# Hybrid encoder trunk: deep projection banks, filled norm gaps, and the recurrent stream and queries in three products

## What is computed

```python
z = x @ w_in                       # columns: rnn stream 1024 | q 1024 | k 128 | v 128 | two gates 2048
A = rglru(causal_conv(z_rnn))      # linear recurrence over tokens
B = banded attention(rope(q), rope(k), v, sinks)
m = sigmoid(g_rnn) * (A @ w_br_rnn) + sigmoid(g_attn) * (B @ w_br_attn)
x = LayerNorm(alpha * x + m @ w_out)
scores = sigmoid(x @ w_router)     # top 8 of 64 experts, in 4 of 8 groups
x = LayerNorm(alpha * x + shared_expert(x) + sum_topk gate_e * expert_e(x))
```

## Time and profile before

| | |
|---|---|
| median of 3 runs | 1719.76 us (1717.3 to 1720.46) |
| the profiled execution | 1717.09 us |
| its span, first to last instruction | 1715.3 us |
| busy in the span | TensorE 96%, VectorE 42%, ScalarE 29% |
| layer 0: first projection product / first recurrent gate product | 15.78 / 95.29 us |
| layer 0: to_tokens / fill / router / gather | 277.54 / 286.61 / 294.33 / 322.22 us |
| layer 1: first projection product | 863.21 us |

### The profile page before, as it was taken

One profiled execution on the slowest core, in us unless ns is written; L12 is line 12 of the kernel. 1 busy time (PEld: TensorE's weight loads), 2 busy tenths in 40 slices (PEclk: granted clock), 3 DMA queues, 4 the chain that ended last, 5 costly groups with the idle time before them and its releaser, 6 DMA issues.

```text
span 1715.3 us, 24854 instructions
## 1 busy us (share of the span) xinstructions
PE 1640.0 (96%) x9230; PEld 1059.5 (62%) x9230; DVE 719.6 (42%) x1543; ACT 495.4 (29%) x1005; POOL 23.2 (1%) x38
## 2 busy tenths in 40 slices
PE   8999998999999999999799999989999999999995
PEld 5667897745545555555477779966555555545543
DVE  3646565333333323423445656562342333333323
ACT  1054434123223222232211544332223223223222
POOL 2000000000000000000010000000000000000000
PEclk9999997999999999999889999979999999999997
DMA  7644466299999999999246425554999999999960
GB/s 194 150 149 146 100 172 227 73 359 391 401 402 407 393 394 409 387 409 400 78 104 203 152 83 140 142 208 170 393 402 396 400 403 401 391 410 396 402 240 30
DMA packets 166339, 476.30 MB, mean 278 GB/s; under 512 B 43252, under 2 KB 99124, under 8 KB 133508
## 3 DMA queue, kind: packets, MB, share of 16 engines
q1 hardware_dynamic: 164480, 472.32, 73.5%
q0 software_dynamic: 1440, 2.98, 0.7%
q10 hardware_dynamic: 356, 0.13, 0.0%
HBM read 473.83 MB, written 1.57 MB: 277 GB/s over the span
## 4 chain that ended last, share of the span: by engine, by line
PE 94%; DVE 2%; ACT 2%; issue 1%; DMA 0%; POOL 0%; SPq 0%; DVEq 0%; ACTq 0%; POOLq 0%
PE ps L793 26%; PE ps L518 17%; PE ps L813 13%; PE ps L834 4%; PE ps L835 4%; PE ps L778 4%; PE ps L779 4%; PE ps L531 3%; PE ps L532 3%; PE ps L533 3%; PE ps L544 2%; PE ps L781 2%; PE ps L822 1%; PE ps L728 1%; DVE stats_of L1226 1%
## 5 line engine op out<-in xcount | busy, mean ns | idle before, releaser
L793 PE MATMUL ps<-experts,xg 128*64 128x512 f32 x2048 | 450.5, 592 | 2.8 <-ACT xg L1073 2.8
L793 PEld LDWEIGHTS ps<-experts,xg 128*64 128x64 f32 x2048 | 148.4, 137 | 293.0 <-issue 293.0
L518 PE MATMUL ps<-xT,dense 128*128 128x288 f32 x1184 | 302.7, 416 | 4.9 <-DVE tmp L1290 4.2
L518 PEld LDWEIGHTS ps<-xT,dense 128*128 128x128 f32 x1184 | 227.5, 194 | 70.3 <-issue 6.8
L813 PE MATMUL ps<-experts,hidT 128*64 128x512 f32 x1024 | 233.8, 598 | 1.8 <-ACT hidT L1087 1.8
L1507 DVE TENSOR_TENSOR hid<-ps,hid 128x256 f32<-128x256 f32 x64 | 27.2, 425 | 388.4 <-ACT hid L1081 388.4
L1095 ACT ACTIVATE yh<-ps,gsl 128x512 fp32r<-128x512 f32 x128 | 88.0, 687 | 228.2 <-PE ps L813 228.2
L1073 ACT ACTIVATE xg<-ps,gperm_all 128x256 f32<-128x256 f32 x256 | 130.6, 561 | 62.8 <-PE ps L781 59.2
L1519 DVE SCALAR_TENSOR_TENSOR yl<-ps,gsl,yh 128x512 fp32r<-128x512 f32 x128 | 96.1, 751 | 124.5 <-ACT yh L1095 124.5
L834 PE MATMUL ps<-ohT,yh 128*128 128x288 f32 x512 | 145.1, 308 | 3.1 <-DVE yl L1519 3.1
L813 PEld LDWEIGHTS ps<-experts,hidT 128*64 128x64 f32 x1024 | 68.5, 136 | 121.6 <-issue 121.6
(11 more groups left out here) (253 smaller groups left out, 1707.6 us busy)
## 6 DMA issues: line engine op xcount, KB each, us to landing
experts<-in_w SPq DMA_DIRECT2D x384, 1024.0 KB, 9.5
dense<-in_w_in SPq DMA_DIRECT2D x26, 1024.0 KB, 5.4
dense<-in_w_in SPq DMA_DIRECT2D x32, 256.0 KB, 4.4
dense<-in_w_br_rnn SPq DMA_DIRECT2D x8, 1024.0 KB, 5.2
dense<-in_w_br_attn SPq DMA_DIRECT2D x16, 512.0 KB, 6.2
dense<-in_w_out SPq DMA_DIRECT2D x8, 1024.0 KB, 5.3
dense<-in_ws SPq DMA_DIRECT2D x6, 1024.0 KB, 5.6
tok<-in_x_prompt SPq DMA_DIRECT2D x1, 1024.0 KB, 5.3
```

Of the source, the lines that this page charges most:

```text
L518: last = mm(bank[:, 0:n], w[:, k, col:col + P], rhs(k), start=k == 0, stop=k == KC - 1)
L793: last = mm(ps[e % 2 * CAP:(e % 2 + 1) * CAP, 2, :], xg[:, k, e * CAP:e * CAP + CAP], experts[:, e, 0:2, k * DE:k * DE + DE], start=k == 0 ...
```

## The change

1. **Banks.** Projection items use `z_bank(i)`: bank i % 6 up to the last query, bank i % 2 from the recurrent gates on. An item waits for item i-6.
2. **Order.** Keys and values go ahead of the queries, in products and in pieces. VectorE turns the keys first; the small tables of layer 0 come after all ropes.
3. **Three products** for stream chunks 2 to 7 and all queries, 14 chunks a layer. Seven pieces more go through `high_parts` and `low_parts`. ScalarE makes `x_hi` and VectorE `x_lo` from `xT` at the start of a layer.
4. **Fills** use all eight banks; only the first two chunks wait.
5. **Router** with the weights stationary: eight products with 288 moving columns, each as soon as its chunk is evicted, a VectorE copy into `lgT`, three transposes back.
6. **Order behind norm 1**: `xh`/`xl` of tiles 0 and 1 around the copy, of tile 2 after the sigmoid and after the gates.
7. **`keep_clock`**: matmuls of the identity by 512 columns whose result is not read: 6 behind `to_tokens(yP)`, 3 behind the last `combine`, 4 behind `to_tokens(ffT)`.

```diff
+FILL = (0, 1, 4, 5, 6, 7, 2, 3)
-Z_RNN, Z_Q, Z_K, Z_V, Z_LRU, Z_GATE, ... = 0, 8, 16, 17, 18, 34, ...
+Z_RNN, Z_K, Z_V, Z_Q, Z_LRU, Z_GATE, ... = 0, 8, 9, 10, 18, 34, ...
+Z_DEEP = 6
-PIECES = ([("in", 256 * j) for j in range(4)] + [("q", j) for j in range(4)] + [("in", K_OFF)]
+PIECES = ([("in", 256 * j) for j in range(4)] + [("in", K_OFF)] + [("q", j) for j in range(4)]
-SPLIT = list(range(D_BR, D_ROUTER))
+SPLIT = list(range(D_IN + 1, D_KV)) + list(range(D_Q, D_G)) + list(range(D_BR, D_ROUTER))
+F_BR = SPLIT.index(D_BR)
+def z_bank(i):
+    return i % Z_DEEP if i < Z_LRU else i % 2
...
             def bank_of(L, i):
-                pe.wait_ge(z_free[i % 2], z_count(L, i))
-                return ps[:, i % 2, :]
+                if Z_DEEP <= i < Z_LRU:
+                    pe.wait_ge(z_free[i % 2], z_count(L, i - Z_DEEP) + 1)
+                elif i >= Z_LRU:
+                    pe.wait_ge(z_free[i % 2], z_count(L, i))
+                return ps[:, z_bank(i), :]
...
             def fill_xT(wait):
                 for c in range(KC):
-                    wait(c)
+                    if c < 2:
+                        wait(c)
                     for t, (at, n) in enumerate(TOK):
-                        last = transpose(ps[:, c % 2, at:at + n], tok[0:n, t, c * P:c * P + P], ident[0:n, 0:n])
+                        last = transpose(ps[:, FILL[c], at:at + n], tok[0:n, t, c * P:c * P + P], ident[0:n, 0:n])
...
+            def keep_clock(bank, n):
+                for _ in range(n):
+                    mm(ps[:, bank, :], ident, cst[:, 0:512], start=True, stop=True)
...
# TensorE, a layer
+                    ready = (lambda k: pe.wait_ge(x_lo_ready, 2 * L + k // 4 + 1)) if m == 2 else None
+                    over_parts(L, bank_of(L, Z_RNN + m), D_IN + m // 2, m % 2 * P, x_hi, x_lo, ready).then_inc(z_ready[m % 2], 1)
...
+                for c in range(KC):
+                    over_parts(L, bank_of(L, Z_Q + c), D_Q + c // 2, c % 2 * P, x_hi, x_lo).then_inc(z_ready[c % 2], 1)
...
                 to_tokens(yP)
+                keep_clock(0, 6)
...
-                for t, (at, n) in enumerate(TOK):
-                    for k in range(KC):
-                        last = mm(ps[0:n, 2, t * NE:t * NE + NE], xT[:, k, at:at + n], w[:, k, :], start=k == 0, stop=k == KC - 1)
+                for k in range(KC):
+                    pe.wait_ge(z_free[k % 2], z_count(L, Z_FILL1 + k) + 1)
+                    last = mm(ps[0:NE, 0, 0:T], w[:, k, :], xT[:, k, :], start=k == 0, stop=k == KC - 1)
+                last.then_inc(logits_T, 1)
+                pe.wait_ge(logits_kept, L + 1)
+                for t, (at, n) in enumerate(TOK):
+                    last = transpose(ps[0:n, 2, t * NE:t * NE + NE], lgT[0:NE, at:at + n], ident[0:NE, 0:NE])
                 last.then_inc(logits, 1)
...
                 round_of(pe.snap(done), meanwhile=shared_down)
+                keep_clock(2, 3)
                 pe.wait_ge(rounds_set, L + 1)
...
                 to_tokens(ffT)
+                keep_clock(0, 4)
...
# ScalarE, a layer
+                for h in range(2):
+                    ...
+                    activation(x_hi[:, c, :], xT[:, c, :], ACT.Copy).then_inc(x_hi_ready, 1)
+                if L == 0:
+                    high_parts(0, 0)
+                high_parts(L, 1)
                 for m in range(KC):
                     bank = z_item(L, Z_RNN + m)
...
+                    if m in (3, 5, 7):
+                        high_parts(L, m // 2 + 1)
...
+                high_parts(L, 5)
+                high_parts(L, 6)
...
                 act.wait_ge(w2_done, FREE + act.snap(done) * 4)
+                if L < depth - 1:
+                    high_parts(L + 1, 0)
                 norm_rows(L, 1)
...
# VectorE, a layer
+                for h in range(2):
+                    ...
+                    V.tensor_tensor(x_lo[:, c, :], xT[:, c, :], as_f(x_hi[:, c, :]), ALU.subtract).then_inc(x_lo_ready, 1)
+                if L == 0:
+                    low_parts(0, 0)
...
                     last.then_inc(u_ready, 1)
+                    if c in (0, 3, 5, 7):
+                        low_parts(L, (0, 3, 5, 7).index(c) + 1)
...
-                for c in range(KC + 1):
-                    i = Z_Q + c
+                for c in range(-1, KC):
+                    i = Z_Q + c if c >= 0 else Z_K
...
+                    if c in (1, 2):
+                        low_parts(L, 4 + c)
+                if L == 0:
+                    decay_rates()
+                    sink_tables()
...
+                keep_low(0)
+                dve.wait_ge(logits_T, L + 1)
+                V.tensor_copy(lgT[0:NE, :], ps[0:NE, 0, 0:T]).then_inc(logits_kept, 1)
+                keep_low(1)
...
                 stats(L, 1, LN_EPS)
+                if L < depth - 1:
+                    low_parts(L + 1, 0)
```

More of the change, by code:

```diff
@@ L238, in build @@
         o_hi, m_hi, h_hi = (parts[:, 2 * _w + j * _t:2 * _w + (j + 1) * _t].rearrange("p (c t) -> p c t", c=KC) for j in range(3))
+        x_hi, x_lo = o_hi, m_hi
         as_f = lambda x: x.bitcast(F32)
@@ L309, in build @@
         xl_ready = sem("xl_ready")
+        logits_T = sem("logits_T")
+        logits_kept = sem("logits_kept")
         logits = sem("logits")
@@ L359, in wait_piece_used @@
             elif kind == "router":
-                eng.wait_ge(logits, L + 1)
+                eng.wait_ge(logits_T, L + 1)
                 return
@@ L559, in _ @@
             pe.wait_ge(x_in, 32)
-            fill_xT(lambda c: pe.wait_ge(z_free[c % 2], c // 2) if c >= 2 else None)
+            fill_xT(lambda c: None)
             pe.wait_ge(vectors_in, VECTOR_DMAS * 16)
             pe.wait_ge(cached_in, CACHED_DMAS * 16)
+            for b in range(2):
+                pe.wait_ge(z_free[b], Z_FIRST)
             for l in range(depth):
-                transpose(ps[:, 2, l * P:l * P + P], raw[:, 0, l, :], ident)
-                last = transpose(ps[:, 3, l * P:l * P + P], raw[:, 1, l, :], ident)
+                transpose(ps[:, 6, l * P:l * P + P], raw[:, 0, l, :], ident)
+                last = transpose(ps[:, 7, l * P:l * P + P], raw[:, 1, l, :], ident)
             last.then_inc(rows_ready, 1)
@@ L578, in _ @@
                 for m in range(KC):
-                    if m % 2 == 0:
-                        piece(L, D_IN + m // 2)
-                    over_features(bank_of(L, Z_RNN + m), D_IN + m // 2, m % 2 * P, xk, T).then_inc(z_ready[m % 2], 1)
-                for c in range(KC):
-                    if c % 2 == 0:
-                        piece(L, D_Q + c // 2)
-                    over_features(bank_of(L, Z_Q + c), D_Q + c // 2, c % 2 * P, xk, T).then_inc(z_ready[c % 2], 1)
+                    if m == 0:
+                        piece(L, D_IN)
+                    if m < 2:
+                        over_features(bank_of(L, Z_RNN + m), D_IN, m % 2 * P, xk, T).then_inc(z_ready[m % 2], 1)
+                        continue
+                    ready = (lambda k: pe.wait_ge(x_lo_ready, 2 * L + k // 4 + 1)) if m == 2 else None
+                    over_parts(L, bank_of(L, Z_RNN + m), D_IN + m // 2, m % 2 * P, x_hi, x_lo, ready).then_inc(z_ready[m % 2], 1)
                 piece(L, D_KV)
@@ L942, in norm_back @@
                 for c in range(0, KC, 2):
-                    bank = z_item(L, first + c)
+                    act.wait_ge(z_ready[0], z_count(L, first + c) + 1)
+                    bank = ps[:, FILL[c], :]
                     activation(xT[:, c, :], bank[:, 0:T], ACT.Identity, bias=prm_all[:, L, b * KC + c:b * KC + c + 1],
@@ L953, in _ @@
             for L in range(depth):
+                for h in range(2):
+                    c = slice(h * 4, h * 4 + 4)
+                    for b in range(2):
+                        act.wait_ge(z_free[b], Z_FIRST - KC // 2 + L * Z_HALF + 2 * h + 2)
+                    activation(x_hi[:, c, :], xT[:, c, :], ACT.Copy).then_inc(x_hi_ready, 1)
+                if L == 0:
+                    high_parts(0, 0)
+                high_parts(L, 1)
                 for m in range(KC):
@@ L1249, in norm_back @@
                 for c in range(1, KC, 2):
-                    bank = z_item(L, first + c)
+                    dve.wait_ge(z_ready[1], z_count(L, first + c) + 1)
+                    bank = ps[:, FILL[c], :]
                     V.tensor_scalar(xT[:, c, :], bank[:, 0:T], prm_all[:, L, g * KC + c:g * KC + c + 1],
@@ L1426, in _, with keep_low @@
                 norm_back(L, V_G1, V_B1, Z_FILL1)
-                for t, (at, n) in enumerate(TOK):
+                def keep_low(t):
+                    n = TOK[t][1]
                     dve.wait_ge(xh_ready, L * NT + t + 1)
```

69 lines of the change are left out of this document (38 added, 31 removed).

## The result

The changed kernel takes 1688.15 us (median of 4 runs, 1684.93 to 1689.34) against 1720.03 for the kernel before on the same chip: ratio 0.9821, 95% interval 0.9809 to 0.9833. The profiled execution took 1684.93 with a span of 1683.0, so 32.3 us of span went. The forecast for the median was 1683.4, within 1671 to 1699. The profiled execution is also the fastest of the four (the spans of the others are 1685.4, 1687.0 and 1687.4), so the gains read from its trace are those of a good execution; e7 tells what the others may lack.

The account below looks back on a forecast made before the run. TensorE, 94% of the span, bounds the kernel, with VectorE becoming the bound in the projection. Gains 9.7 + 4.1 + 15.6 + 7.0 = 36.4 off 1717.09 give 1680.7, plus 2.7 for the median: 1683.4 us, range 1671 to 1699.

Parts of the forecast that it names:

- Rates: Projection: a chunk takes 3.20 us in three products against 3.88 in float32, a rope 2.85, a piece's low part 2.4.
- Projection, layer 0: Up to the recurrent gates: VectorE becomes the bound, gates end at 97.7 against 107.44, gaining 9.7 us.
- The rival that TensorE stays the bound: Projection: the ropes keep up with TensorE, worth at most 9 us more, giving 1674; chance 0.12.
- The table load: Recurrent gates: the load now lies in the wait, so the first pair takes about 1.3 us instead of 2.6.
- Projection, layer 1: Up to the recurrent gates: 79.5 us after against 83.6 before, gaining 4.1 (bounds 0 and 9.5).
- Norm 1: Norm 1 to gather: dummies, faster fill and router bring gather 8.8 us earlier, less 1.0 for the clock: 7.8 a layer.
- The clock rival: Norms: the clock is not held, so norm 1 loses 4.4 us and norm 2 1.6 each, giving 1693; chance 0.20.
- Norm 2, layer 0: Four dummies against 4.36 us idle and a fill of 2.8 to 5.1 instead of 6.95: gain taken as 3.5 us.
- Norm 2, layer 1: The last fill gains the same 3.5 us, with 24 transposes behind it that gain if the clock holds.
- The three dummies: Norm 2, ahead of the register reading: queued while control code runs, they cost nothing; in line they would cost 2 x 2.6 us.
- The start: Before layer 0's first product: the faster first fill is worth 0 to 0.3 us, taken as 0.
- Slower rival (ring): Projection: ScalarE, VectorE, TensorE and loads wait on each other in a ring, 3.5 us a piece, giving 1732; chance 0.05.

Follow-up runs that it names:

- e7: The changed kernel run once more, nothing edited: 1690.67 us, ratio 0.9843 to the kernel before.
- e2: The changed kernel with the four rotating VectorE operations left out of each rope, so attention is computed from wrong queries and keys: 1678.1 us, ratio 0.9763.
- e3: The changed kernel with the first query piece's high part behind the evictions of stream chunks 6 and 7, and low parts later: 1689.17 us, ratio 0.9827.
- e6: The changed kernel with stream chunks 2 to 7 and queries back in float32, without their high and low parts: 1695.38 us, ratio 0.9868.
- e5: The changed kernel with seven dummy matmuls instead of four behind to_tokens in norm 2: 1681.27 us, ratio 0.9787.
- e4: The changed kernel with each fill's transposes in two groups of four chunks, eight of 128 rows then four of 32: 1677.77 us, ratio 0.9762.
- e1: The changed kernel without its 13 dummy matmuls a layer: 1695.7 us, ratio 0.9869.
- e11: The kernel with late high parts, grouped fills and seven dummies in both norms, minus the three dummies ahead of the register reading: 1672.41 us, ratio 0.9728.
- e8: The changed kernel with later high parts, grouped fills, and seven dummies in norm 1 (was six) and norm 2 (was four): 1672.02 us, ratio 0.9734.
- e9: The changed kernel with seven dummies instead of six behind to_tokens(yP) in norm 1: 1684.25 us, ratio 0.9797.

## Why the prediction was right, point by point

- **Rates.** 3.20 us a chunk in three products, 2.85 a rope (84.81 - 81.95 = 2.86), 2.36 a pair of low parts: as taken.
- **Projection, layer 0: right.** Forecast 9.7, measured 10.4 up to `to_tokens(yP)`. VectorE was to be the bound, and TensorE to stop for 5.3 us with two products between; it stopped from 81.7 to 87.2, and e2 shows what lies behind it. Counted from the first product the gates end at 81.3, forecast 81.9. One term was mis-sized: VectorE's wait for the first query piece, forecast 3, was 5.46. It hardly moved the end (ropes done 70.6 behind the first product, forecast 70.0), since VectorE would otherwise have waited for TensorE (e3). The 1.5 for a low clock in the gates was about right: their clock was 0.50 from 88 to 90, and they lost 1.1 (e6). The rival that TensorE stays the bound is refuted by e2.
- **The table load: right.** ScalarE loads the sigmoid's table for 1.28 us at 71.86, in its wait, and the first sigmoid begins at 85.19, when the first product is done (84.42 + 0.73). With the drain that the Trainium skill counts beside a load ("ScalarE: Activation LUTs", "What ACT_TABLE_LOAD costs") the gain would have been 1.4 larger a layer; layer 1 gave 4.0 against my 4.1, so the trace does not show it. Nor does the kernel before, where the eviction ahead of the load ended at 95.93 and the sigmoid stands right behind it:

```profile
95.95 1.28 ACT L965 ACT_TABLE_LOAD   x1
97.24 0.90 ACT L965 ACTIVATE B<-ps,prm_all 128x291 f32<-128x291 f32 x2
```

- **Projection, layer 1: right**, 4.0 for 4.1, though both ends of the difference were 1.6 to 1.7 too low: the gates end 85.2 behind the first product before and 81.2 after, forecast 83.6 and 79.5. The sum left out that the first products of layer 1 run at half clock in either kernel; e5, where they do not, has 79.7. By e6 the products give 4.6.
- **Norm 1: right sum by luck, two wrong terms.** "If the clock stays high the fill takes 2.8, as the 24 transposes at 277.54 do" failed: it takes 4.42 at full clock. Those transposes all have 128 rows; in a fill every third has 32, and e4 shows that the changes between them cost 1.6 us. The routing chain started 10.9 behind the fill's start (288.43 - 277.54), forecast 9.7. Against this stood the 1.0 that I took off for a falling clock: in the profiled execution it did not fall. The two misses cancel, and the measured 7.9 and 7.3 lie next to the forecast 7.8. Where the clock does fall it takes 2.9, not 1.0. The wait ahead of the ranks was 0.72 (forecast 1.2), and `sel` came 7.14 behind the chain's start.
- **The clock rival: half true.** Forecast as one case of 0.20 for all executions; it is a matter of each norm 1 of each execution, and its price (2.9) is below the 4.4 I gave it. By one of its own signs of being wrong, a clock of 0.50 in the router, the prediction stands for the profiled execution and not for one like e7's, where the window from 282 shows 0.50. The rival probably carries the difference between the profiled 1684.93 and the median (e7).
- **Norm 2, layer 0: nearly right for a wrong reason.** I set 3.4 us of dummies against 4.36 idle. But 4.36 belonged to transposes that had run at half clock, with a stall between them; in layer 1 of the kernel before, where they ran at full clock, it was 6.25 (the fence under e4). From the start of `to_tokens` to the fill VectorE and ScalarE need 9.1 us whenever the transposes run at full clock: 9.07 in rows 10 (286.61 - 277.54), 9.10 here (836.24 - 827.14). The idle time is then 6.26, four dummies leave 2.82, and the clock falls inside the fill: 6.05, and the first chunk of layer 1 is slow as well. What did gain was `to_tokens`: with the register gap 6.7 us (823.27 to 829.98) against some 10.7 before, since the clock held and the stall of 1.76 inside it is gone. Of the two only the clock can be the dummies' doing: e1 and e11, without the three, show no stall there either, and e6, with them, shows one of 0.74.
- **Norm 2, layer 1: wrong**, 0.8 for 3.5, the largest miss and most of the 4.1 by which the sum of 36.4 exceeds the 32.3 of the profile. I let layer 0's figure stand for both. The last `to_tokens` had no stall to lose, the clock fell in the fill (5.75), and the 24 transposes behind it took 5.36 as before. Seven dummies bring the 3.9 back (e5).
- **The three dummies: right.** In layer 0 `to_tokens` begins 3.87 us behind the start of the dummies (827.14 - 823.27) instead of 3.35 behind the combine, so of their 2.7 only 0.5 lies in line, and e11 shows that even this is none. By the rule of the Trainium skill that other instructions queue while control code runs ("Advanced Engine Details and Errata", "Sequencer Loop") they would cost nothing; the trace agrees.
- **The start: forecast 0, measured -1.3.** 0.6 is the landing of x (first transpose at 8.63 against 8.02) and varies between executions: the first product stood at 16.65 to 17.35 in the eight kernels with the alternating fill. The other 0.64 is a wait of the four transposes of vectors for all eight evictions, which used to be spread. In e4 and e8 that wait is still there (0.88 and 0.79), but ends so early that the first product waits for the landing of the first piece instead (1.50 and 0.62).
- **Slower rival (ring): refuted.** No row shows TensorE waiting for `dense_lo` or `parts` in the projection, and the experts keep their 507.1 us in either layer (from their first product to the first of the last `combine`; 507.2 in layer 1 after the change).

## What to carry to other kernels

When TensorE gets cheaper products, add up the next engine's work over the same stretch first: here the wait for VectorE and the clock that fell in it took nearly half of the saving (e6), and leaving VectorE's rotation out gives 6.4 us a layer (e2). Size a filler for an idle stretch by how long the other engines need at full clock, not by the idle time seen after a slow stretch, and leave as little as possible open: with 1.1 us left open the clock fell in 7 of 12 cases, at 2.9 us each, and with 0.25 in none. And group transposes of equal shape.

## What the runs showed of the hardware

- 24 transposes took 4.42 us with shapes of 128 and 32 rows in turn and 2.77 grouped, both at a granted clock of 1.00; 24 of 128 rows take 2.81. At 0.50, 24 transposes with shapes in turn took 6.95 and 24 of 128 rows 5.36.
- The same program at the same place kept its clock in one norm and lost it in the next (e7); with 1.11 us of idleness ahead of an alternating fill it held 5 times of 12. With 0.25 it held 12 times of 12 (e5's norm 2 and e9's norm 1, four alternating fills; e8 and e11, eight grouped ones). With 2.82 it fell inside every fill, alternating or grouped, mostly after its first transposes.
- Three dummies (2.7 us) issued ahead of a register reading cost no time (e8 against e11: 0.00 us apart over 528 in layer 0; in layer 1 the run with them is 0.5 shorter).
